# High-weight products of both weight tiles first, then the low-weight products of both

## The reference

```python
z = h @ w_in                                   # first block: conv, q, k, v, gates
mix = (sigmoid(g_a) * ya + sigmoid(g_b) * yb) @ w_out
u = peer_u[ec]; a = gelu(einsum("ckd,cd->ck", u, hc)) * gc; out = einsum("ck,ckd->cd", a, peer_v[ec])
z = h @ w_in[l]                                # second block: recurrent, linear attention, memory
proj = einsum("bsnc,ncd->bsnd", branches, w_branch[l])
x = x + (gelu(gate_h) * val_h) @ w_down[l]     # gate_h, val_h from h2 @ w_up[l]
```

## Time and profile before

| | |
|---|---|
| Median of 3 runs | 1577.75 us (1576.43 to 1579.17) |
| The profiled execution | 1575.39 us |
| Its span | 1573.3 us |
| TensorE matmul busy | 1559.8 us (99%) |
| TensorE weight load busy | 1471.2 us (94%) |
| VectorE busy | 1070.1 us (68%) |
| GpSimd busy | 883.9 us (56%) |
| ScalarE busy | 880.9 us (56%) |
| Granted TensorE clock | full speed in all 40 slices |

### The profile page before, as it was taken

One profiled execution on the slowest core, in us unless ns is written; L12 is line 12 of the kernel. 1 busy time (PEld: TensorE's weight loads), 2 busy tenths in 40 slices (PEclk: granted clock), 3 DMA queues, 4 the chain that ended last, 5 costly groups with the idle time before them and its releaser, 6 DMA issues.

```text
span 1573.3 us, 33476 instructions
## 1 busy us (share of the span) xinstructions
PE 1559.8 (99%) x12568; PEld 1471.2 (94%) x12568; DVE 1070.1 (68%) x1867; ACT 880.9 (56%) x1251; POOL 883.9 (56%) x413
## 2 busy tenths in 40 slices
PE   9999999999999999999999999999999999999998
PEld 8999899999999999998888888889999999999998
DVE  7998743879933777778888766676937484455522
ACT  6566765554454444444444445557677654676653
POOL 8786468968886000000000244457876689898886
PEclk9999999999999999999999999999999999999999
DMA  6564335555555555555555665556543356565553
GB/s 223 171 197 157 107 123 188 192 183 190 191 183 196 176 163 183 173 167 170 185 177 170 218 195 193 196 200 189 173 143 107 118 170 190 192 199 188 189 196 124
DMA packets 86217, 277.03 MB, mean 176 GB/s; under 512 B 11232, under 2 KB 18160, under 8 KB 86128
## 3 DMA queue, kind: packets, MB, share of 16 engines
q1 hardware_dynamic: 85712, 274.76, 53.7%
q0 software_dynamic: 272, 1.05, 0.2%
q10 hardware_dynamic: 144, 0.00, 0.0%
HBM read 274.73 MB, written 1.05 MB: 175 GB/s over the span
## 4 chain that ended last, share of the span: by engine, by line
PE 92%; issue 2%; DVE 2%; POOL 2%; ACT 2%; DMA 0%; SPq 0%; DVEq 0%; ACTq 0%; POOLq 0%
PE gemm L679 35%; PE gemm L996 22%; PE gemm L698 18%; PE aux L1282 4%; PE gemm L827 3%; PE aux L976 2%; POOL w_lo L466 1%; PE gemm L714 1%; PE gemm L739 1%; ACT w_hi L1378 1%; PE gemm L1282 1%; PE aux L946 0%; PE gemm L813 0%; PE gemm L720 0%; PE gemm L756 0%
## 5 line engine op out<-in xcount | busy, mean ns | idle before, releaser
L466 POOL TENSOR_TENSOR w_lo<-raw,w_hi 128x1024 fp32r<-128x1024 f32 (+1 forms) x330 | 789.8, 2402 | 279.9 <-ACT w_hi L1378 275.8
L1378 ACT ACTIVATE w_hi<-raw 128x1024 fp32r<-128x1024 f32 (+1 forms) x492 | 514.7, 1048 | 556.8 <-PE gemm L679 310.4
L679 PE MATMUL gemm<-h_lo,w_hi 128*128 128x256 f32 x2144 | 504.7, 277 | 0.0
L679 PE MATMUL gemm<-h_hi,w_hi 128*128 128x256 f32 x2096 | 499.8, 279 | 1.1 <-ACT w_hi L1378 1.0
L679 PEld LDWEIGHTS gemm<-h_lo,w_hi 128*128 128x128 f32 x2144 | 402.8, 188 | 0.7 <-issue 0.2
L679 PEld LDWEIGHTS gemm<-h_hi,w_hi 128*128 128x128 f32 x2096 | 394.3, 188 | 3.8 <-issue 1.6
L698 PE MATMUL gemm<-h_hi,w_lo 128*128 128x256 f32 x2096 | 284.6, 277 | 2.4 <-POOL w_lo L466 1.5
L698 PEld LDWEIGHTS gemm<-h_hi,w_lo 128*128 128x128 f32 x2096 | 259.8, 188 | 4.9 <-POOL w_lo L466 3.4
L466 DVE TENSOR_TENSOR w_lo<-raw,w_hi 128x1024 fp32r<-128x1024 f32 x162 | 195.5, 1221 | 100.6 <-ACT w_hi L1378 99.5
L996 PE MATMUL gemm<-w_hi,act_parts 128*128 128x512 f32 x1008 | 247.9, 386 | 0.4 <-ACT act_parts L1579 0.4
L996 PEld LDWEIGHTS gemm<-w_hi,act_parts 128*128 128x128 f32 x1008 | 187.6, 187 | 36.6 <-issue 0.5
(11 more groups left out here) (436 smaller groups left out, 2175.9 us busy)
## 6 DMA issues: line engine op xcount, KB each, us to landing
raw<-in_w_u SPq DMA_DIRECT2D x128, 512.0 KB, 3.5
raw<-in_w_ev SPq DMA_DIRECT2D x128, 512.0 KB, 3.6
raw<-in_w_up SPq DMA_DIRECT2D x48, 512.0 KB, 3.5
raw<-in_w_gate SPq DMA_DIRECT2D x24, 512.0 KB, 3.8
raw<-in_w_down SPq DMA_DIRECT2D x24, 512.0 KB, 3.5
raw<-in_w_conv_in SPq DMA_DIRECT2D x16, 512.0 KB, 4.3
raw<-in_w_peer_q SPq DMA_DIRECT2D x16, 512.0 KB, 3.8
raw<-in_w_branch SPq DMA_DIRECT2D x24, 288.0 KB, 2.8
```

Source lines behind the costliest of these rows:

```text
L466: eng.tensor_tensor(w_lo[v][:, 0:n], raw[c.raw][v][:, 0:n], w_hi[v][:, 0:n], ALU.subtract).then_inc(lo_ready[v], 1)
L679: return pe.matmul(spread(out), w[:, k, :], spread(x[n][:, k, :]), start=(n == k == 0), stop=False)
L1378: act.activation(w_hi[v][:, 0:n], raw[c.raw][v][:, 0:n], ACT.Copy).then_inc(hi_ready[v], 1)
```

## The change

The edit replaces the body of `product` alone. It takes all high-weight matmuls of tile 0, then those of tile 1, then the low-weight matmuls of tile 0, then those of tile 1. The same 48 matmuls on the same operands are issued, with the same four semaphore waits and the same four increments (`hi_used[0]`, `hi_used[1]`, `tile_done[0]`, `tile_done[1]`). The accumulation start flag stands on the first matmul of the chunk only, as in `paced_product`. `product_tile` is unchanged where it is called alone. No other engine's program changes.

```diff
             def product(c, m, it=None, x=(h_hi, h_lo), steps=KD):
 
+                bank_free(c, it)
+                chunks = 0 if it is None else it * BANKS
+                both = pair(gemm[c.bank], m)
                 for v in range(2):
-                    product_tile(c, v, m, it, x, steps)
+                    pe.wait_ge(hi_ready[v], chunks + (c.split + 1))
+                    w = by_k(w_hi[v], m, n=steps)
+                    for k in range(steps):
+                        for n in range(2):
+                            mm = pe.matmul(spread(both[:, v, :]), w[:, k, :], spread(x[n][:, k, :]),
+                                           start=(v == k == n == 0), stop=False, skip_group_check=True)
+                    mm.then_inc(hi_used[v], 1)
+                for v in range(2):
+                    pe.wait_ge(lo_ready[v], chunks + (c.split + 1))
+                    w = by_k(w_lo[v], m, n=steps)
+                    for k in range(steps):
+                        mm = pe.matmul(spread(both[:, v, :]), w[:, k, :], spread(x[0][:, k, :]), start=False,
+                                       stop=(k == steps - 1), skip_group_check=True)
+                    mm.then_inc(tile_done[v], 1)
```

## The result

| | median, us | runs | lowest to highest |
|---|---|---|---|
| before | 1577.77 | 8 | 1575.41 to 1579.17 |
| changed | 1581.96 | 8 | 1579.96 to 1583.48 |

The ratio is 1.0028, with a 95% interval of 1.0018 to 1.0037: 4.2 us slower, where the prediction had 3.1 (1580.9, range 1577.0 to 1586.5).

A forecast was written before the change was run, and what follows sets the result against it. The prediction took TensorE, busy for 99% of the span, to bound the kernel. Waits won (-1.8 us) and lost (+4.9) gave net +3.1, so 1577.75 + 3.1 = 1580.9 us, range 1577.0 to 1586.5.

The follow-up runs named there:

- e6: The changed kernel with POOL subtracting the first 224 columns of tile 1 twice in the first half of `u`: 1589.85 us, 1.0068 against the kernel before.

## What to carry to other kernels

When a reordering turns a buffer's reserve into waiting time saved elsewhere, cost the places where the steady cycle ends: the first chunk of another shape, the first behind a crowd, the last ahead of one. A reserve that is spent in the chunk before is missed there, and putting back the old order at that place alone comes too late. In a cycle with a fixed amount of slack, an excess costs only each second turn, as the 0.38 us of e6 did, because the turn that waited hands its delay on as slack.

## What the runs showed of the hardware

- The same matmuls ran at 114.3 or 116.7 ns each (256 columns), 223.3 or 226.7 (512 columns), at a granted clock of 1.00, for hundreds in a row. The pace of 256-column stretches differed between two executions of one kernel (`v` and `down`); that of `ev` differed between programs alone. A stretch of 560 matmuls is worth 1.3 us of it.
- A DVE operation of 0.43 us on two SBUF operands took 2.50 us when POOL's subtraction had begun before it, 1.40 when that was cut in half, and ended 0.28 us after POOL's. An addition with one operand in PSUM took its 0.68 us beside such a subtraction.
- A POOL subtraction costs 0.19 us of its own and 2.14 ns per column: 48 columns took 0.29 us, 224 took 0.67.
- The first load of the program took 5.08 us in one execution of the kernel before and 6.19 in the other, and their first 19 us differ by 2.3.
